# Reordering the opening of a two-block transformer kernel: zero products first, half-unit weights, meta tokens turned raw

## The chip, the cores and the metric

The kernel runs on one core of a Trainium2 chip. The metric is the device time of one execution in microseconds (us). The profiled execution also has a span, the time from its first to its last instruction.

## The reference

Two transformer blocks run over 256 tokens of width 1024. Only the start of the first block matters here: 16 meta tokens are put ahead of the 256 tokens of x, the 272 rows are normed, and the result is multiplied by the weight matrix `w_in`.

```
h = concatenate([meta_tokens, x])          # 16 + 256 rows of 1024
a = h * rsqrt(mean(h*h, axis=-1) + EPS) * norm1
proj = a @ w_in                            # u, q, k, v of two attentions, forget gates
...                                        # pool mixer, two attentions, w_out, gated FFN
                                           # then the second block: FFN, convolution + mLSTM, FFN
```

## The kernel before

**Arithmetic.** Every float32 product with a large weight is made from two parts. A value is rounded to fp32r (its "hi" part), and what is left is its "lo" part. A result is hi·hi + hi·lo + lo·hi, three passes of TensorE. So weights are held as `raw`, `whi`, `wlo` and the activations as `xa`, with the hi part of a 128-column block `kt` at `xa[:, kt, 0:272]` and its lo part at `xa[:, kt, 272:544]`.

**Weights.** All large weights stream in as 1 MB units of 128 x 2048, each of which holds two output tiles (a = 0, 1) of eight 128 x 128 blocks, ordered by kt and then a. There are three slots. SyncE's queue loads a unit into `raw[slot]` once `lo_ready` says that the unit before it in that slot is split. ScalarE writes `whi` (`split`, L608), VectorE subtracts to get `wlo` (L911), TensorE uses both. `unit_used` counts units that TensorE is done with.

**The opening.** SyncE's queue issues x in two parts, the identity, the meta tokens, the vectors of gains, unit 0, `small` (gate and pool weights), unit 1, the constants, unit 2 (L547 to L555). ScalarE squares each part of x with a running sum and takes the root, VectorE scales the identity by 1/rms (`diag`, L963), and TensorE multiplies x by that diagonal, which turns x and norms it in one product (`turn_first`). That is a plain float32 product of 128 columns, which shows as two records in the trace. The meta tokens are squared on VectorE (L967) and turned in the same way with a 16 x 16 diagonal `diag_m`: eight small products, each behind the turn of one kt of the second part of x. Each kt has a PSUM bank of its own. Then ScalarE writes the hi part of `xa` with the gain `norm1` (L706), and VectorE the lo part (L984). VectorE alone splits unit 0: a cast to `whi` (L973), the lo part of tile 0 (L978, `half_ready`), and, after the lo parts of `xa`, the lo part of tile 1 (`lo_ready`).

**The first unit.** TensorE takes the work in the order of the list `FIRST`: tile 0 (`proj` 0) with `columns_tile`, three products of 272 columns for each kt, each kt behind its `xa_ready`; tile 1; then `gates` (24 small-weight products, which wait for `small_lo_ready`), then tiles 2 and 3 of unit 1, and so on. ScalarE copies an even tile out of PSUM bank 0, VectorE an odd one out of bank 1. All products are issued by one helper, `mm`, whose line is L1325.

## Time and profile before

| | |
|---|---|
| median of 3 runs | 844.18 us |
| lowest, highest run | 840.53, 844.36 us |
| profiled execution, its time | 842.73 us |
| its span | 840.9 us |
| mean granted TensorE clock | 0.986 |
| TensorE, VectorE, ScalarE busy | 97%, 64%, 51% |

1.83 us of the profiled execution's time lie outside its span. The granted clock is a share of TensorE's full 2.4 GHz, so 0.50 is 1.2 GHz. A busy TensorE isn't TensorE at its peak, since matmuls are pipelined and weight loads (PEld) lie beside them.

### The profile page before, as it was taken

Reading aid. Unit: us, or ns where it says so; the run is one execution under the profiler, and the core shown is the slowest. Engines: PE = TensorE matmul, PEld = TensorE weight load, DVE = VectorE, ACT = ScalarE, POOL = GpSimd, SP = SyncE. Lnnn points to the kernel's source line nnn. Section 1 sums busy time; section 2 is a strip of 40 time slices with the busy share of each in tenths; the row PEclk is TensorE's granted clock in tenths of the full one; section 3 lists DMA queues with packets and bytes.
Section 4 is the critical chain, followed back from the end, with each engine's and each line's share of the span. In section 5 each row is a group of like instructions: output and inputs, shape, how many; then the busy total and the mean of one; then the engine's idle time right before and its main releaser. Section 6 shows DMA issues by size and latency. Waiting matters only on the chain.

```text
span 840.9 us, 12339 instructions
## 1 busy us (share of the span) xinstructions
PE 815.0 (97%) x4807; PEld 715.3 (85%) x4807; DVE 538.0 (64%) x633; ACT 427.5 (51%) x553; POOL 19.7 (2%) x24
## 2 busy tenths in 40 slices
PE   6999997999999999999999999999999999999997
PEld 6989886888888888988888888899887988888886
DVE  5664523676665666786656665876778776666665
ACT  5356542754444445854444446635445754454444
POOL 0000000000000000000000000000440000000000
PEclk8999987999999999999999999999999999999999
DMA  6632122265555455465554554432335555555431
GB/s 259 253 121 101 57 95 100 98 226 183 194 200 193 176 183 196 141 237 196 200 185 176 189 198 163 163 151 101 114 137 201 178 218 184 194 200 193 175 131 50
DMA packets 20653, 141.07 MB, mean 168 GB/s; under 512 B 2432, under 2 KB 2688, under 8 KB 4112
## 3 DMA queue, kind: packets, MB, share of 16 engines
q1 hardware_dynamic: 20048, 138.56, 45.3%
q0 software_dynamic: 576, 2.10, 0.7%
q8 instruction: 21, 0.34, 0.2%
q14 instruction: 8, 0.07, 0.0%
HBM read 139.60 MB, written 1.05 MB: 167 GB/s over the span
## 4 chain that ended last, share of the span: by engine, by line
PE 85%; DVE 7%; ACT 4%; issue 2%; POOL 1%; DMA 1%; DVEq 0%; SPq 0%; ACTq 0%
PE ps L1325 84%; DVE wlo L911 2%; ACT whi L608 1%; PE ps L1331 1%; DMA ident<-ident_in 1%; DVE arena L1292 0%; DVE x L1090 0%; ACT squared L623 0%; DVE xa L922 0%; DVE sb_parts L1074 0%; PE ps L1526 0%; DVE arena L1072 0%; POOL arena L591 0%; DVE arena L1302 0%; ACT arena L879 0%
## 5 line engine op out<-in xcount | busy, mean ns | idle before, releaser
L1325 PE MATMUL ps<-xa,whi 128*128 128x512 f32 (+2 forms) x1808 | 505.0, 348 | 0.8 <-DVE ytmp L1262 0.8
L1325 PE MATMUL ps<-xa,wlo 128*128 128x256 f32 (+1 forms) x1408 | 395.3, 283 | 0.0
L911 DVE TENSOR_TENSOR wlo<-raw,whi 128x2048 fp32r<-128x2048 f32 x128 | 294.1, 2298 | 103.1 <-ACT whi L608 103.0
L1325 PEld LDWEIGHTS ps<-xa,whi 128*128 128x128 f32 x1808 | 315.8, 190 | 45.5 <-issue 3.0
L1325 PEld LDWEIGHTS ps<-xa,wlo 128*128 128x128 f32 x1408 | 267.0, 190 | 1.1
L608 ACT ACTIVATE whi<-raw 128x2048 fp32r<-128x2048 f32 x128 | 244.2, 1908 | 12.1 <-PE ps L1325 11.9
L1325 PE MATMUL ps<-whi,hhi 128*128 128x512 f32 x240 | 93.8, 391 | 0.0
L1325 PE MATMUL ps<-whi,hlo 128*128 128x512 f32 x240 | 93.7, 390 | 0.0
L1325 PE MATMUL ps<-wlo,hhi 128*128 128x512 f32 x240 | 93.5, 390 | 0.0
L794 ACT ACTIVATE hhi<-arena 128x512 fp32r<-128x512 f32 x30 | 19.0, 633 | 89.0 <-PE ps L1325 82.5
L780 ACT ACTIVATE arena<-ps 128x512 f32<-128x512 f32 x33 | 19.7, 596 | 87.5 <-PE ps L1325 87.3
L1325 PE MATMUL ps<-whi,ya 128*128 128x512 f32 x176 | 58.4, 406 | 1.5 <-DVE arena L1254 1.5
L788 ACT ACTIVATE arena<-ps 128x512 f32<-128x512 f32 x33 | 19.7, 596 | 73.1 <-PE ps L1325 73.1
L1325 PEld LDWEIGHTS ps<-whi,hlo 128*128 128x128 f32 x240 | 45.1, 188 | 9.8
L1325 PEld LDWEIGHTS ps<-whi,hhi 128*128 128x128 f32 x240 | 45.1, 188 | 9.6
L1325 PEld LDWEIGHTS ps<-wlo,hhi 128*128 128x128 f32 x240 | 45.1, 188 | 8.5
L1132 DVE TENSOR_TENSOR arena<-ps,arena 128x512 f32<-128x512 f32 x33 | 22.8, 690 | 41.6 <-ACT arena L780 41.6
L1141 DVE TENSOR_TENSOR arena<-ps,arena 128x512 f32<-128x512 f32 x33 | 22.8, 690 | 38.7 <-ACT arena L788 38.6
L1153 DVE TENSOR_TENSOR hlo<-arena,hhi 128x512 fp32r<-128x512 f32 x30 | 20.8, 693 | 38.4 <-ACT hhi L794 38.4
L1325 PEld LDWEIGHTS ps<-whi,ya 128*128 128x128 f32 x176 | 34.0, 193 | 8.9 <-DVE arena L1254 1.8
L1325 PE MATMUL ps<-wlo,ya 128*128 128x512 f32 x88 | 35.1, 399 | 0.0
L1325 PE MATMUL ps<-arena 128*64 128x256 f32 (+9 forms) x180 | 25.6, 337 | 0.8 <-DVE arena L1023 0.5
(190 smaller groups left out, 531.3 us busy)
## 6 DMA issues: line engine op xcount, KB each, us to landing
raw<-wstream SPq DMA_DIRECT2D x129, 1024.0 KB, 4.8
gain_row<-rows_in POOLq DMA_DIRECT2D x4, 512.0 KB, 4.2
x<-x_in SPq DMA_DIRECT2D x2, 512.0 KB, 4.0
out<-x SPq DMA_DIRECT2D x4, 256.0 KB, 2.1
xg<-const_in SPq DMA_DIRECT2D x1, 840.0 KB, 9.4
small<-small_in SPq DMA_DIRECT2D x1, 152.0 KB, 5.8
ident<-ident_in SPq DMA_DIRECT2D x1, 64.0 KB, 4.4
arena<-meta_in SPq DMA_DIRECT2D x1, 64.0 KB, 4.4
```

Source lines behind the costliest of these rows:

```text
L608: nc.scalar.activation(whi[slot][:], raw[slot][:], ACT.Copy).then_inc(hi_ready, 1)
L780: nc.scalar.activation(silu, products(4)[1], ACT.Copy).then_inc(gate_lo_out, 1)
L788: nc.scalar.activation(up_sum, products(6)[1], ACT.Copy).then_inc(up_lo_out, 1)
L794: nc.scalar.activation(ya[:, 0:2, 0:SEQ] if last else hhi[:], hact, ACT.Copy).then_inc(hhi_done, 1)
L911: nc.vector.tensor_tensor(wlo[slot][:], raw[slot][:], whi[slot][:].bitcast(F32), ALU.subtract).then_inc(lo_ready, 1)
L1132: nc.vector.tensor_tensor(silu, products(4)[0], silu, ALU.add).then_inc(gate_out, 1)
L1141: nc.vector.tensor_tensor(up_sum, products(6)[0], up_sum, ALU.add).then_inc(up_out, 1)
L1153: nc.vector.tensor_tensor(lo, hact, hi.bitcast(F32), ALU.subtract).then_inc(hlo_done, 1)
L1325: return nc.tensor.matmul(o, lhsT, rhs, start=start, stop=stop, skip_group_check=True)
L1331: ins = nc.tensor.transpose(turn_place(k, kt)[:, tt * P:(tt + 1) * P], x[:, tt, kt * P:(kt + 1) * P], ident[:])
```

## The change

- Before anything else TensorE makes 12 float32 products of 128 columns from a buffer of zeros (`vn[0][:, 0]`), which VectorE now clears second. Their result, in PSUM bank 0, isn't read.
- The meta tokens are turned raw, as eight transposes into one bank, right behind the zeros. VectorE multiplies them by `norm1` in one instruction, and later, in one instruction for hi and two for lo, by their 1/rms. That reaches all partitions through one product of ones with `diag_m` (`meta_spread`).
- The scaled identities are made by ScalarE, not by VectorE. The turned x lies in banks 3 to 6, two kt to a bank; `norm_turned` now counts pairs of kt.
- SyncE's queue issues the meta tokens ahead of the identity, unit 0 in two halves (kt 0 to 3, kt 4 to 7, both tiles in each), and unit 2 ahead of the constants. VectorE splits each half.
- `first_unit` replaces the first two calls of `columns_tile`: the products with the hi part of `xa` for both tiles first (kt 0 to 3, then kt 4 to 7), those with its lo part last.
- `small` is split ahead of unit 1 on both engines.

Declarations of semaphores are left out of the diff.

```diff
@@ -311,6 +311,9 @@
         xm = carve(at, D)[0:META, :]
...
         diag_m = carve(at, META)[0:META, :]
+        meta_gained = carve(at, KT, META)
+        meta_scaled = carve(at, KT, META)
+        ones_first = carve(at, P)[0:META, :]
         at = [0]
         qT = [carve(at, PAIRS, SEQ) for _ in range(2)]
@@ -512,6 +522,10 @@
             else:
                 engine.wait_ge(m_taken[n % 2], n // 2 + 1)
+        def first_turn_place(kt):
+            return ps[:, 3 + kt // 2, kt % 2 * SEQ:(kt % 2 + 1) * SEQ]
         def in_place(what, s, j):
             if what == "k":
@@ -545,14 +559,15 @@
         def _(sp):
...
                 sp.dma_start(x[:, tt, :], x_in[tt * P:(tt + 1) * P, :]).then_inc(x_landed[tt], 16)
+            sp.dma_start(xm, meta_in).then_inc(meta_landed, 16)
             sp.dma_start(ident[:], ident_in).then_inc(ident_landed, 16)
-            sp.dma_start(xm, meta_in).then_inc(meta_landed, 16)
             sp.dma_start(vecs[:], vecs_in).then_inc(vecs_landed, 16)
-            sp.dma_start(raw[0][:], wstream[0]).then_inc(landed[0], 16)
+            sp.dma_start(raw[0][:, 0:UNIT // 2], wstream[0, :, 0:UNIT // 2]).then_inc(half_landed, 16)
+            sp.dma_start(raw[0][:, UNIT // 2:UNIT], wstream[0, :, UNIT // 2:UNIT]).then_inc(landed[0], 16)
             sp.dma_start(small[:], small_in).then_inc(small_landed, 16)
             sp.dma_start(raw[1][:], wstream[1]).then_inc(landed[1], 16)
+            sp.dma_start(raw[2][:], wstream[2]).then_inc(landed[2], 16)
             sp.dma_start(const_raw, const_in).then_inc(const_landed, 16)
-            sp.dma_start(raw[2][:], wstream[2]).then_inc(landed[2], 16)
             with sp.Fori(1, UNITS // SLOTS) as turn:
                 for s in range(SLOTS):
@@ -650,7 +665,7 @@
             def hi_of(k, gain, tiles):
                 for kt in tiles:
-                    act.wait_ge(norm_turned, KT + 4 * k + turn_group(kt) + 1)
+                    act.wait_ge(norm_turned, KT // 2 + 4 * k + turn_group(kt) + 1)
                     nc.scalar.activation(xa[:, kt, 0:SEQ], turn_place(k, kt), ACT.Copy, scale=vec(gain, kt)).then_inc(xa_hi_ready, 1)
             def root_of_x(p, tt):
@@ -697,18 +712,20 @@
                 act.wait_ge(x_landed[tt], 16)
...
                 root(1, tt, False)
+                act.wait_ge(root_ready, tt + 1)
+                act.wait_ge(ident_landed, 16)
+                nc.scalar.activation(diag[:, tt, :], ident[:], ACT.Copy, scale=stat[:, 20 + tt:21 + tt]).then_inc(diag_ready, 1)
             act.wait_ge(meta_squared, 1)
...
             for kt in range(KT):
-                act.wait_ge(norm_turned, kt + 1)
-                nc.scalar.activation(xa[:, kt, 0:TOK], ps[:, kt, 0:TOK], ACT.Copy,
+                act.wait_ge(norm_turned, kt // 2 + 1)
+                nc.scalar.activation(xa[:, kt, META:TOK], first_turn_place(kt), ACT.Copy,
                                      scale=vec("norm1", kt)).then_inc(xa_hi_ready, 1)
-            split(1, 1, 0)
             act.wait_ge(small_landed, 16)
             nc.scalar.activation(small_hi[:], small[:, 0:W_POOL], ACT.Copy).then_inc(small_hi_ready, 1)
+            split(1, 1, 0)
             for kind, i in FIRST:
                 b45 = 4 + i % 2
@@ -952,43 +969,53 @@
             nc.vector.memset(eps[:], EPS).then_inc(eps_set, 1)
+            nc.vector.memset(vn[0][:, 0, :], 0.0).then_inc(zeros_set, 1)
+            nc.vector.memset(ones_first, 1.0).then_inc(ones_set, 1)
             nc.vector.memset(kT[1][:, :, TOK:3 * P], 0.0)
             nc.vector.memset(fneg, 0.0)
-            nc.vector.memset(vn[0][:, 0, :], 0.0)
             nc.vector.memset(vn[1][:, 2, :], 0.0)
-            dve.wait_ge(ident_landed, 16)
-            def diagonal(tt):
-                dve.wait_ge(root_ready, tt + 1)
-                nc.vector.tensor_scalar(diag[:, tt, :], ident[:], stat[:, 20 + tt:21 + tt], None, ALU.mult).then_inc(diag_ready, 1)
-            diagonal(0)
             dve.wait_ge(meta_landed, 16)
...
                                            accum_out=stat[0:META, 30:31]).then_inc(meta_squared, 1)
-            diagonal(1)
+            dve.wait_ge(meta_turned, 1)
+            dve.wait_ge(vecs_landed, 16)
+            norm1 = vec("norm1", 0, KT).unsqueeze(2).broadcast_to([P, KT, META])
+            nc.vector.tensor_tensor(meta_gained, ps[:, 7, 0:KT * META].rearrange("p (k m) -> p k m", k=KT), norm1, ALU.mult)
+            def first_hi_part(n):
+                part = slice(n * UNIT // 2, (n + 1) * UNIT // 2)
+                dve.wait_ge(landed[0] if n else half_landed, 16)
+                nc.vector.tensor_copy(whi[0][:, part], raw[0][:, part]).then_inc(first_hi, 1)
+            def first_lo_part(n):
+                part = slice(n * UNIT // 2, (n + 1) * UNIT // 2)
+                dve.wait_ge(first_hi, n + 1)
+                nc.vector.tensor_tensor(wlo[0][:, part], raw[0][:, part], whi[0][:, part].bitcast(F32),
+                                        ALU.subtract).then_inc(lo_ready if n else half_ready, 1)
+            first_hi_part(0)
+            first_lo_part(0)
+            dve.wait_ge(ident_landed, 16)
             dve.wait_ge(root_ready, 3)
             nc.vector.tensor_scalar(diag_m, ident[0:META, 0:META], stat[0:META, 32:33], None, ALU.mult).then_inc(diag_ready, 1)
-            dve.wait_ge(landed[0], 16)
-            link(nc.vector.tensor_copy(whi[0][:], raw[0][:]))
-            def rest_of_first(a):
-                part = lambda w: w.rearrange("p (k a n) -> p k a n", k=KT, a=2)[:, :, a, :]
-                return nc.vector.tensor_tensor(part(wlo[0][:]), part(raw[0][:]), part(whi[0][:].bitcast(F32)), ALU.subtract)
-            rest_of_first(0).then_inc(half_ready, 1)
-            dve.wait_ge(vecs_landed, 16)
+            first_hi_part(1)
+            dve.wait_ge(meta_spread, 1)
+            meta_rstd = ps[:, 2, 0:META].unsqueeze(1).broadcast_to([P, KT, META])
+            nc.vector.tensor_tensor(xa[:, :, 0:META], meta_gained, meta_rstd, ALU.mult).then_inc(xa_meta_ready, 1)
+            link(nc.vector.tensor_tensor(meta_scaled, meta_gained, meta_rstd, ALU.mult))
+            nc.vector.tensor_tensor(xa[:, :, TOK:TOK + META], meta_scaled, xa[:, :, 0:META].bitcast(F32),
+                                    ALU.subtract).then_inc(xa_meta_ready, 1)
+            first_lo_part(1)
             for kt in range(KT):
-                dve.wait_ge(xa_hi_ready, kt + 1)
-                nc.vector.scalar_tensor_tensor(xa[:, kt, TOK:2 * TOK], ps[:, kt, 0:TOK], vec("norm1", kt),
-                                               xa[:, kt, 0:TOK].bitcast(F32), ALU.mult,
+                dve.wait_ge(xa_hi_ready, kt // 2 * 2 + 2)
+                nc.vector.scalar_tensor_tensor(xa[:, kt, TOK + META:2 * TOK], first_turn_place(kt), vec("norm1", kt),
+                                               xa[:, kt, META:TOK].bitcast(F32), ALU.mult,
                                                ALU.subtract).then_inc(xa_ready, 1)
-            rest_of_first(1).then_inc(lo_ready, 1)
-            split(1, 1)
             dve.wait_ge(small_hi_ready, 1)
...
                                     ALU.subtract).then_inc(small_lo_ready, 1)
+            split(1, 1)
             for kind, i in FIRST:
                 b45 = 4 + i % 2
@@ -1104,7 +1131,7 @@
             def normed_x():
                 dve.wait_ge(gain_landed, 16)
-                dve.wait_ge(norm_turned, KT + 4 + turn_group(KT - 1) + 1)
+                dve.wait_ge(norm_turned, KT // 2 + 4 + turn_group(KT - 1) + 1)
                 for tt, h in HALVES:
...
                     nc.vector.scalar_tensor_tensor(half(x, tt, h), half(x, tt, h), stat[:, 8 + tt:9 + tt],
@@ -1347,11 +1374,9 @@
                     ins = mm(ps[:, bank, tt * P:(tt + 1) * P], ones, diag[:, tt, :], True, True)
                 ins.then_inc(rstd_spread, 1)
-            def columns_tile(o, slot, a, n, first_wait=None, skip=0):
+            def columns_tile(o, slot, a, n, skip=0):
                 for kt in range(KT):
-                    if first_wait is not None:
-                        pe.wait_ge(xa_ready, first_wait + kt + 1)
                     w = slice(kt * 256 + a * P, kt * 256 + (a + 1) * P)
...
                     mm(o, whi[slot][:, w], xa[:, kt, n + skip:2 * n], False, False)
@@ -1441,16 +1466,61 @@
                 return ins
-            def turn_first(tt, kt):
-                return mm(ps[:, kt, META + tt * P:META + (tt + 1) * P], x[:, tt, kt * P:(kt + 1) * P], diag[:, tt, :], True, True)
+            def turn_first(tt, tiles):
+                for kt in tiles:
+                    ins = mm(first_turn_place(kt)[:, tt * P:(tt + 1) * P], x[:, tt, kt * P:(kt + 1) * P], diag[:, tt, :], True, True)
+                    if tt and kt % 2:
+                        ins.then_inc(norm_turned, 1)
+            def first_unit():
+                def product(kt, a, part, lo, stop=False):
+                    w = slice(kt * 256 + a * P, kt * 256 + (a + 1) * P)
+                    return mm(ps[:, a, 0:TOK], part[0][:, w], xa[:, kt, lo * TOK:(lo + 1) * TOK], kt == 0 and part is whi and not lo, stop)
+                pe.wait_ge(xa_meta_ready, 1)
+                pe.wait_ge(half_ready, 1)
+                for kt in range(KT // 2):
+                    pe.wait_ge(xa_hi_ready, kt + 1)
+                    for part in (whi, wlo):
+                        for a in range(2):
+                            product(kt, a, part, 0)
+                pe.wait_ge(first_hi, 2)
+                for kt in range(KT // 2, KT):
+                    pe.wait_ge(xa_hi_ready, kt + 1)
+                    for a in range(2):
+                        product(kt, a, whi, 0)
+                pe.wait_ge(lo_ready, 1)
+                for kt in range(KT // 2, KT):
+                    for a in range(2):
+                        product(kt, a, wlo, 0)
+                pe.wait_ge(xa_meta_ready, 2)
+                for kt in range(KT - 1):
+                    pe.wait_ge(xa_ready, kt + 1)
+                    for a in range(2):
+                        product(kt, a, whi, 1)
+                pe.wait_ge(xa_ready, KT)
+                product(KT - 1, 0, whi, 1, True).then_inc(even_full, 1)
+                product(KT - 1, 1, whi, 1, True).then_inc(unit_used, 1)
+            pe.wait_ge(zeros_set, 1)
+            for _ in range(12):
+                mm(ps[:, 0, 0:P], vn[0][:, 0, 0:P], vn[0][:, 0, P:2 * P], True, True)
+            pe.wait_ge(meta_landed, 16)
+            pe.wait_ge(ident_landed, 16)
+            for kt in range(KT):
+                ins = nc.tensor.transpose(ps[:, 7, kt * META:(kt + 1) * META], xm[:, kt * P:(kt + 1) * P], ident[0:META, 0:META])
+            ins.then_inc(meta_turned, 1)
             pe.wait_ge(diag_ready, 1)
-            for kt in range(KT):
-                turn_first(0, kt)
+            turn_first(0, range(KT))
+            pe.wait_ge(diag_ready, 2)
+            turn_first(1, range(KT // 2))
+            pe.wait_ge(ones_set, 1)
             pe.wait_ge(diag_ready, 3)
-            for kt in range(KT):
-                turn_first(1, kt)
-                mm(ps[:, kt, 0:META], xm[:, kt * P:(kt + 1) * P], diag_m, True, True).then_inc(norm_turned, 1)
+            mm(ps[:, 2, 0:META], ones_first, diag_m, True, True).then_inc(meta_spread, 1)
+            turn_first(1, range(KT // 2, KT))
             for kind, i in FIRST:
                 pair = 6 + i % 2
@@ -1460,16 +1530,13 @@
                     n = U_IN + i // 2
...
                     if i == 0:
-                        pe.wait_ge(half_ready, 1)
-                    if i == 1:
-                        pe.wait_ge(xa_ready, KT)
-                        pe.wait_ge(lo_ready, 1)
+                        first_unit()
                     if i >= 2:
...
                         wait_tiles(pe, i - 2)
-                    skip = META if query else 0
-                    columns_tile(ps[:, i % 2, skip:TOK], n % SLOTS, i % 2, TOK, 0 if i == 0 else None,
-                                 skip).then_inc(unit_used if i % 2 else even_full, 1)
+                        skip = META if query else 0
+                        columns_tile(ps[:, i % 2, skip:TOK], n % SLOTS, i % 2, TOK,
+                                     skip).then_inc(unit_used if i % 2 else even_full, 1)
                 if kind == "gates":
...
```

## Rows read from the trace of the kernel before

**Rows 1.** The profile's page: busy time, share of the span, instructions.

```profile
PE 815.0 (97%) x4807; PEld 715.3 (85%) x4807; DVE 538.0 (64%) x633; ACT 427.5 (51%) x553; POOL 19.7 (2%) x24
```

**Rows 2.** Waits of TensorE, whole span: us in total, times, longest.

```profile
PE ps L1325 <- DVE sb_parts L1074: 7.2, 3, 4.7
PE ps L1325 <- DVE diag L963: 6.5, 1, 6.5
```

**Rows 3.** Windows: length, PE, PEld, DVE, ACT, POOL busy, PEclk, DMA share, GB/s.

```profile
6.47:14.60 8.13, 8.13 (x39) 7.15 (x39) 6.10 (x10) 3.79 (x11) 0.00 (x0) 1.00 1.01 417
14.70:21.40 6.70, 6.70 (x27) 6.14 (x28) 4.58 (x6) 4.77 (x7) 0.00 (x0) 0.50 0.17 53
21.50:25.20 3.70, 3.70 (x32) 3.70 (x31) 3.20 (x3) 0.86 (x2) 0.00 (x0) 1.00 0.96 385
105.00:110.00 5.00, 3.94 (x21) 3.94 (x22) 1.34 (x2) 0.11 (x1) 0.00 (x0) 0.68 0.46 187
```

**Rows 4.** Timeline of the opening, VectorE: start, length, what.

```profile
1.68 0.38 DVE L957 MEMSET arena<- 128x384 f32 x1
...
6.13 0.29 DVE L963 TENSOR_SCALAR diag<-ident,stat 128x128 f32<-128x128 f32 x1 [3.66 <-DMA ident<-ident_in]
...
6.50 1.21 DVE L967 SCALAR_TENSOR_TENSOR arena<-arena 16x1024 f32<-16x1024 f32 x1
...
7.66 0.27 DVE L963 TENSOR_SCALAR diag<-ident,stat 128x128 f32<-128x128 f32 x1
...
8.96 1.23 DVE L973 CAST whi<-raw 128x2048 fp32r<-128x2048 f32 x1 [0.42 <-DMA raw<-wstream]
10.22 1.22 DVE L978 TENSOR_TENSOR wlo<-raw,whi 128x1024 fp32r<-128x1024 f32 x1
...
13.29 0.50 DVE L984 SCALAR_TENSOR_TENSOR xa<-ps,vecs,xa 128x272 fp32r<-128x272 f32 x1 [0.24 <-ACT xa L706]
```

**Rows 5.** Timeline of the opening, TensorE: turning x and the meta tokens.

```profile
6.47 4.21 PE L1325 MATMUL ps<-diag,x 128*128 128x128 f32 x18 [6.47 <-DVE diag L963]
...
11.92 0.49 PE L1325 MATMUL ps<-diag,x 128*128 128x128 f32 x2
...
12.34 0.39 PE L1325 MATMUL ps<-arena 16*128 16x16 f32 x2
...
15.01 0.80 PE L1325 MATMUL ps<-diag,x 128*128 128x128 f32 x2
...
15.73 0.60 PE L1325 MATMUL ps<-arena 16*128 16x16 f32 x2
...
17.53 0.82 PE L1325 MATMUL ps<-xa,whi 128*128 128x272 f32 x2
```

**Rows 6.** Timeline, TensorE: products of the first unit, then the gates.

```profile
18.15 0.43 PE L1325 MATMUL ps<-xa,wlo 128*128 128x272 f32 x1
...
18.83 0.43 PE L1325 MATMUL ps<-xa,wlo 128*128 128x272 f32 x1
...
22.27 0.29 PE L1325 MATMUL ps<-xa,wlo 128*128 128x272 f32 x1
...
24.14 0.29 PE L1325 MATMUL ps<-xa,wlo 128*128 128x272 f32 x1
...
25.27 0.21 PEld L1325 LDWEIGHTS ps<-xa,small_hi 128*6 128x6 f32 x2
```

**Rows 7.** Timeline and lines: turns by transpose, 6 and 128 rows.

```profile
34.31 0.31 PE L1481 MATMUL ps<-ident,arena 6*128 6x6 f32 x3
...
L1526 PE MATMUL ps<-ident,arena 128*128 128x128 f32 x8 | 1.1, 279 | 0.6 <-ACT arena L739 0.6
```

**Rows 8.** DMA issues: size in KB, median us to landing.

```profile
ident<-ident_in SPq DMA_DIRECT2D x1, 64.0 KB, 4.4
```

**Rows 9.** Timeline: what VectorE does as the first unit ends.

```profile
22.42 2.28 DVE L911 TENSOR_TENSOR wlo<-raw,whi 128x2048 fp32r<-128x2048 f32 x1
...
25.59 0.44 DVE L1023 COPY arena<-ps 128x272 f32<-128x272 f32 x1 [0.89 <-PE ps L1325]
```

More of the change, by code:

```diff
@@ L407, in build_blocks @@
         meta_squared = sem("meta_squared")
+        zeros_set = sem("zeros_set")
+        ones_set = sem("ones_set")
+        half_landed = sem("first_half_unit_landed")
+        first_hi = sem("first_unit_hi_ready")
+        meta_turned = sem("meta_turned")
+        meta_spread = sem("meta_rstd_spread")
+        xa_meta_ready = sem("xa_meta_columns_ready")
         diag_ready = sem("diag_ready")
```

## The prediction

> **What bounds the kernel now.** I read the page first. TensorE is busy for 97% of the span [rows 1], so anything that ends a stretch of TensorE earlier moves the end of the kernel, provided nothing later hangs on another clock. Next the waits of TensorE: over the whole span they hold two large entries, 7.2 us in the attention of the first block and 6.5 us in the very first wait, for the scaled identity [rows 2]. Only the second is in the reach of this change. Third, the windows of the opening. The reader is to look at PEclk, the granted clock: it is 1.00 up to 14.6 us, 0.50 from 14.7 to 21.4 and 1.00 again from 21.5 [rows 3]. So the opening has two losses: TensorE idle until 6.47, and then 6.8 us at 1.2 GHz in which it was busy all the time. What did it do before the clock fell? It had idled for 6.5 us, and then made float32 products of 128 columns, at last mixed with 16 x 16 ones [rows 5]. Before the clock rose it had made products of 272 columns from 17.53 on [rows 5]. A later fall, between 105 and 110 us, follows a wait [rows 2, 3]. So both thin work and idling precede falls here, and the rows can't say which of them made the one at 14.65.
>
> The point at which I compare is the first weight load of the gates, at 25.27 [rows 6]. From there on TensorE has the same list of work.
>
> **What TensorE's opening becomes.** I write the new order out with prices of the rows.
>
> *Zeros.* The clear of the zero buffer starts at 1.68 now, and two clears of about 0.4 us stand ahead of it that move behind it. So it starts at 0.9, lasts 0.38 [rows 4] and lets TensorE go at 1.3. A float32 product of 128 columns is two records; 18 records took 4.21 us [rows 5], so a product costs 0.468 at the full clock. 12 x 0.468 = 5.6: the zeros end at 6.95. They are no longer under cover to their end: the first scaled identity was ready at 6.42 [rows 4], so some 0.5 us of them is on the path. Bounds for one product are 0.42 (a turn up to the meta product behind it, 12.34 - 11.92) and 0.72 (the same at the lower clock, 15.73 - 15.01) [rows 5].
>
> *Meta tokens raw.* Eight transposes of 16 rows. Meta tokens and identity now leave the queue third and fourth, so the identity is due some 0.45 us later than its 6.1 (it took 4.4 from issue [rows 8]), before 6.95. The trace has three transposes of 6 rows in 0.31 us and eight of 128 rows in 1.1 [rows 7]; I take 0.8 for the eight, since the 16-row ones resemble the first, with 1.1 as the upper bound. End: 7.75.
>
> *Turns of x.* 16 x 0.468 = 7.5, and one small product for the spread of the meta roots, 0.39 (the pair of meta records, with its tail [rows 5]). Seven such products are gone. End of turning: 7.75 + 7.5 + 0.39 = 15.6, against 17.53. ScalarE makes both identities; VectorE had them at 6.4 and 7.9 [rows 4]. On ScalarE the second comes behind the square of the second x tile and a wait for its own root, which I put at 9.0, and TensorE asks for it at 11.5. Cover 2.5 us.
>
> *Products of the first unit.* Two tiles of 24 before, 32 + 16 now: 48 either way. At the full clock the products from 22.27 to 24.14 are 15, so 0.125 each; at the lower one three take 0.68, so 0.227 [rows 6]. 48 x 0.125 = 6.0. End: 21.6.
>
> Sum: 25.27 - 21.6 = 3.6 us earlier. About 2.9 of that is clock. Between 17.53 and 21.45 some 17.3 products cost 0.10 too much each, 1.8 us; and of the 2.9 us of turning after 14.65, 1.1 is clock, by the lengths 0.80 + 0.60 against 0.49 + 0.39 [rows 5]. The other 0.7 is reordered work. So the change lives on whether the clock stays up.
>
> **Are the operands there?** The products want the hi parts of `xa`. ScalarE can make kt 0 to 3 from about 12.6 on, as their pairs are turned, and kt 6 and 7 by 16.7, while TensorE asks for kt 6 at about 18.1. VectorE: square of the meta tokens 6.1 to 7.35 (1.21 [rows 4]); their gain at 7.8, when TensorE has turned them; the first half of unit 0, landed before the whole of it at 8.96, cast in 0.6 (half of 1.23) and its remainder in 1.22 [rows 4], by 10.0; second half cast by 10.9. Then VectorE waits for `meta_spread`. That is a new wait: TensorE gets to it only at 13.8, and behind it on VectorE stand the second half's lo part and all lo parts of `xa`. Three small instructions bring it to 14.5, the lo part (1.22) to 15.7, eight lo parts of `xa` at 0.5 each [rows 4] to 19.7. TensorE wants the second half's lo part at 18.6, and the last lo part of `xa` at 15.6 + 46 x 0.125 = 21.4. Slack 1.7 us. Price if the cover were gone: VectorE's lateness one for one.
>
> **What follows it.** The gates need `small_lo`, which comes right behind, at 20.1. Splitting unit 1 then ends on VectorE at 22.4, tile 2 starts at 24.6. VectorE splits unit 2 until 24.7, as now (22.42 + 2.28), so its copy of the odd tile comes at 24.7 instead of 25.59 [rows 9]; tile 3 needs bank 1 at 27.5. Slack 2.8. ScalarE's copy of tile 0 moves from inside the unit to its end, 21.7, and bank 0 is wanted at 24.6. SyncE's queue has one issue more, but the transfers run at 417 GB/s through 14.6 us [rows 3], so bytes and not issues set the landings; the constants land one unit later and are read by ScalarE near 29. Unit 3 is asked for when unit 0 is split, 15.7 instead of 20. I cost all of these at nothing, and give each a chance below only through VectorE.
>
> **A rule weighed.** The Trainium skill ("TensorE: Matmul & The Clock Gate", Part 1) says that the default state is the lower clock and that activity releases it. This trace disagrees at the start: the first products, after 6.5 us of idling, ran at 1.00. By the rule the zeros would warm the clock up; by the row there is nothing to warm, and the zeros can only keep. The skill also says there (Part 4) that transposes in TensorE's transpose mode don't count as busy in the same way; it speaks against putting the eight of them ahead of the turns, and no row here shows it.
>
> **Against the runs.** The profiled execution took 842.73, span 840.9. The four executions shown (844.36, 844.18, 840.53, 842.73) average 842.95, and their spread of 3.8 is as large as the gain. I take 842.95 - 3.6 = 839.3. That is 4.9 under the median of 844.18, 0.58%. A measurement of this kernel tells about 0.5% (4.2 us) from no change, so the forecast stands just past the bound.
>
> **The rivals.**
> - *The clock still falls near the end of the turning*, as at 14.65. For: the turns stay thin work, and thin work stood right before the fall. Against: the 16-column products, the thinnest, are gone from there, and there is no idling ahead. Price: the last 0.95 us of turning is 1.54 times as long (0.72 / 0.468), 0.5; then the products run for 3.95 us at the lower clock, as from 17.53 to 21.45, 17.4 of them at 0.10 too much, 1.8. Gain 3.6 - 2.3 = 1.3: 841.6. If it falls at 12.1 the gain is gone: 843.
> - *VectorE becomes the bound* through the wait for `meta_spread`. For: five jobs are queued behind it. Against: 1.7 us of slack. If its small instructions and waits cost 2.7 more than I think, 1.0 is lost: 840.3.
> - *The lower clock from the first zeros on.* One mechanism, slower: a product of zeros, or a program whose first act is thin work at 1.3 us, draws the fall to the start. Zeros 12 x 0.72 to 9.9, transposes 1.6, turns 11.5, spread 0.6: 23.6; 3.95 us of products at 0.227, then 30.6 at 0.125: 31.4. That is 6.1 late: 849.1. It is slower than before once the fall comes ahead of 12.1, and measurably so ahead of about 4. For: idling and thin work precede the falls. Against: thin work from 6.47 to 10.6 ran at 1.00 [rows 3, 5]. By the rule of the skill cited above, a start at the lower clock is the default.
>
> **Chances.** Clock stays up, 839.3: 0.55. Late fall, 841.6: 0.25. VectorE, 840.3: 0.10. Fall near 12, no change: 0.06. Lower clock from the start, 849.1: 0.04. The range runs from the lowest run shown less the gain (840.53 - 3.6 = 836.9) to the fall near 12 (843.0). Price bounds lie inside: zeros at 0.42 give 0.6 more, transposes at 1.1 take 0.3. Against the median, faster by over 0.5% means under 839.96. The first case does it in some 0.63 of its executions' spread (0.35), the second seldom (0.05), the third in half (0.05): 0.45. Slower by over 0.5%: 0.04. The rest, 0.51, lies within.
>
> **What the new profile would show.** Windows: PEclk 1.00 from 0 to 22; a 0.50 there is one of the clock rivals, and its start says which. Timeline of TensorE: zeros 1.3 to 6.95, first product of unit 0 at 15.6, first gate load at 21.6. Waits: none of TensorE on VectorE between 15 and 22. The prediction is wrong if the first gate load comes at 21.6 and the time doesn't follow; then a later fall of the clock, shifted or added, has taken it back.

## Result: 834.76 us against 844.27, ratio 0.9891, and the profile after

Four runs each gave a median of 834.76 us (831.78 to 835.33) for the changed kernel and 844.27 (840.53 to 844.65) for the one before: ratio 0.9891, 95% interval 0.9862 to 0.9919, so 7 to 12 us less by the interval. I had forecast 839.3, at least 836.9. The profiled execution took 835.33 with a span of 833.1. The direction was right, and the gain that I had forecast at the gates was less than half of what came.

The first thing to read is again the first weight load of the gates. This is the timeline of the changed kernel on TensorE up to there (start, length, what):

```profile
1.36 5.44 PE L1352 MATMUL ps<-arena 128*128 128x128 f32 x24 [1.36 <-DVE arena L972]
6.72 0.67 PE L1514 MATMUL ps<-ident,arena 16*128 16x16 f32 x8
7.32 2.94 PE L1352 MATMUL ps<-diag,x 128*128 128x128 f32 x24
10.47 0.36 PE L1352 MATMUL ps<-arena 16*128 16x16 f32 x2 [0.21 <-DVE arena L1001]
10.76 1.16 PE L1352 MATMUL ps<-diag,x 128*128 128x128 f32 x8
11.68 0.49 PE L1352 MATMUL ps<-xa,whi 128*128 128x272 f32 x2
...
15.78 2.16 PE L1352 MATMUL ps<-xa,whi 128*128 128x272 f32 x16
17.77 0.41 PE L1352 MATMUL ps<-xa,small_hi 128*6 128x272 f32 x2
```

The gates' products begin at 17.77; in the timeline the products of the kernel before begin at 25.39, 0.12 behind the weight load of [rows 6]. That is 7.6 us earlier, where I had 3.6. The terms of the sum: zeros to 6.8 (I had 6.95), transposes 0.67 (0.8), unit 0 in 6.0 us (6.0). The turns are the odd one. 24 records took 2.94 us and 8 took 1.16 with its tail, 0.122 a record, so 0.245 for a turn (two records). I had 0.468, nearly twice that. And the zeros, the same kind of product, did take 0.453 each.

The windows of the changed kernel (columns as in [rows 3]):

```profile
0.00:25.00 25.00, 23.44 (x174) 22.14 (x175) 17.39 (x33) 16.07 (x30) 0.86 (x5) 1.00 0.87 330
95.00:110.00 15.00, 12.82 (x81) 12.04 (x81) 7.15 (x9) 4.86 (x8) 0.00 (x0) 0.77 0.24 94
120.00:135.00 15.00, 10.29 (x46) 8.73 (x46) 7.00 (x8) 2.82 (x3) 0.00 (x0) 0.66 0.20 70
```

PEclk is 1.00 through the opening: the fall at 14.65 is gone, as the first case of the forecast had it. Two later falls, of which [rows 3] show one for the kernel before, are still there.

The waits of TensorE up to 20 us (us in total, times, longest):

```profile
PE ps L1352 <- DVE arena L972: 1.4, 1, 1.4
PE ps L1352 <- DVE arena L1001: 0.2, 1, 0.2
```

The 6.5 us of [rows 2] have become 1.4, for the cleared buffer, and there is a new wait of 0.2 for `diag_m` (L1001). The timeline of VectorE in the changed kernel shows where that comes from:

```profile
8.24 0.69 DVE L989 CAST whi<-raw 128x1024 fp32r<-128x1024 f32 x1 [0.49 <-DMA raw<-wstream]
8.97 1.23 DVE L994 TENSOR_TENSOR wlo<-raw,whi 128x1024 fp32r<-128x1024 f32 x1
10.11 0.22 DVE L1001 TENSOR_SCALAR arena<-ident,stat 16x16 f32<-16x16 f32 x1
10.25 0.67 DVE L989 CAST whi<-raw 128x1024 fp32r<-128x1024 f32 x1
...
11.60 1.22 DVE L994 TENSOR_TENSOR wlo<-raw,whi 128x1024 fp32r<-128x1024 f32 x1
12.73 3.22 DVE L1012 SCALAR_TENSOR_TENSOR xa<-ps,vecs,xa 128x256 fp32r<-128x256 f32 x8
15.87 0.33 DVE L1016 TENSOR_TENSOR small_lo<-small,small_hi 128x176 fp32r<-128x176 f32 x1
...
20.52 0.43 DVE L1050 COPY arena<-ps 128x272 f32<-128x272 f32 x1
```

`diag_m` stands behind the cast and the remainder of the first half. The last lo part of `xa` is there at 15.95, and its product runs near 17.6: the slack of 1.7 us, as forecast.

**Where the factor of two was.** In the opening the length of a weight load tells the clock better than PEclk does. Here are the groups of weight loads, by shape, in four stretches (count, busy us, mean ns). First the kernel before, 6.47 to 10.5 us:

```profile
L1325 PEld LDWEIGHTS ps<-diag,x 128*128 128x128 f32 x18 | 3.9, 330 | 6.5 <-DVE diag L963 6.5
```

The same kernel, 11.1 to 14.5:

```profile
L1325 PEld LDWEIGHTS ps<-diag,x 128*128 128x128 f32 x10 | 1.5, 192 | 0.1
```

The changed kernel, zeros (1.36 to 6.3), then turns (7.3 to 11.5):

```profile
L1352 PEld LDWEIGHTS ps<-arena 128*128 128x128 f32 x24 | 5.2, 331 | 1.4 <-DVE arena L972 1.4
```

```profile
L1352 PEld LDWEIGHTS ps<-diag,x 128*128 128x128 f32 x31 | 3.6, 191 | 0.1
```

A weight load of 128 columns takes 330 ns at first and 191 ns later, in both kernels, and 1.00 is what PEclk shows for all four stretches. 330 is the length that goes with 1.2 GHz, as the kernel before shows between 17.7 and 21.3, where PEclk is 0.50 and recorded:

```profile
L1325 PEld LDWEIGHTS ps<-xa,whi 128*128 128x128 f32 x12 | 3.3, 327 | 0.0
```

So TensorE began at the lower clock in both kernels, and the 1.00 ahead of the first recorded change isn't a measurement. The clock records kept in the two traces say the same: the first one, of the full clock, begins at 11.25 us in the kernel before and at 6.62 in the changed one, and for the time ahead of it there is none. PEclk counts time without a record as 1.00.

The trace of the kernel before also held the price of such a product at the full clock, in a later stretch that I hadn't looked at, behind several recorded changes. Two float32 products of 128 columns (four records) stand there one behind the other:

```profile
172.60 0.61 PE L1325 MATMUL ps<-diag,exact 128*128 128x128 f32 x4
```

That is 0.31 us a product at most, with the tail of the last one in it.

### The profile page after: what moved, and what is told of

The parts are those of the page before. It is cut to its first block, busy times and chain, and to the rows that moved or that the text cites. A ratio compares the mean times of both kernels' runs of the same rounds, so it can differ in the third digit from the quotient of the medians.

```text
span 833.1 us, 12387 instructions
## 1 busy us (share of the span) xinstructions
PE 812.1 (97%) x4825; PEld 713.6 (86%) x4825; DVE 537.7 (65%) x637; ACT 428.0 (51%) x555; POOL 19.7 (2%) x24
## 4 chain that ended last, share of the span: by engine, by line
PE 85%; DVE 7%; ACT 4%; issue 2%; POOL 1%; DMA 1%; SPq 0%; DVEq 0%; ACTq 0%
PE ps L1352 84%; DVE wlo L928 2%; ACT whi L623 1%; PE ps L1358 1%; DMA raw<-wstream 1%; DVE arena L1319 0%; DVE x L1117 0%; ACT squared L638 0%; DVE xa L939 0%; DVE sb_parts L1101 0%; PE ps L1593 0%; DVE arena L1099 0%; POOL arena L606 0%; DVE arena L1329 0%; ACT arena L896 0%
## 5 line engine op out<-in xcount | busy, mean ns | idle before, releaser
L1352 PE MATMUL ps<-arena 128*64 128x256 f32 (+10 forms) x190 | 27.5, 349 | 2.3 <-DVE arena L972 1.4
```

What stands on the lines that cost most here:

```text
L1352: return nc.tensor.matmul(o, lhsT, rhs, start=start, stop=stop, skip_group_check=True)
```

## The experiments

All times are medians of several runs; ratios are against the kernel before, run on the same chip in turn. "Gates" is the first weight load of the gates in the profiled execution (25.27 before; 17.66 in the changed kernel, 0.11 ahead of the product above). Five profiled executions whose opening is in effect that of the changed kernel (the changed one twice, 9, 11, 13) have it between 17.59 and 17.84, so a difference under 0.3 us at the gates says little.

**1. No zeros.** The changed kernel without its opening products.

```diff
-            for _ in range(12):
-                mm(ps[:, 0, 0:P], vn[0][:, 0, 0:P], vn[0][:, 0, P:2 * P], True, True)
```

> The changed kernel without its 12 products of zeros. Theory (TensorE was at the lower clock in its first products in both kernels, whatever PEclk shows, and the zeros take that time out of the turns): weight loads of 333 ns in the first turns; transposes 1.3 us instead of 0.67, some six turns at 0.455 us and ten at 0.245, so the turning ends near 13.4 instead of 11.68 and the gates begin near 19.4 instead of 17.77; if the clock then falls as it did in the kernel before, up to 3 us more, so 21 to 22.5. Rival (the turns became fast by themselves, because nothing stands between them any more): turns at 0.245 from the first on, gates at 17.8 or a little earlier, time equal to that of the changed kernel.

Measured: 837.50 us, ratio 0.9934 (0.9912 to 0.9955). The weight loads of the turns between 7.6 and 11 us:

```profile
L1352 PEld LDWEIGHTS ps<-diag,x 128*128 128x128 f32 x16 | 3.5, 330 | 0.0
```

They were slow again. Turning ended at 13.60, gates at 19.58, PEclk stayed 1.00. The theory holds, the rival falls. The zeros are worth 1.9 us at the gates. They cost nothing there: without them TensorE starts its transposes at 6.72, as in the changed kernel, because the identity isn't there earlier.

```profile
6.72 1.00 PE L1512 MATMUL ps<-ident,arena 16*128 16x16 f32 x8 [6.72 <-DMA ident<-ident_in]
```

**2. Zeros only.** The kernel before with the zeros alone.

```diff
             nc.vector.memset(eps[:], EPS).then_inc(eps_set, 1)
+            nc.vector.memset(vn[0][:, 0, :], 0.0).then_inc(zeros_set, 1)
...
-            nc.vector.memset(vn[0][:, 0, :], 0.0)
...
+            pe.wait_ge(zeros_set, 1)
+            for _ in range(12):
+                mm(ps[:, 0, 0:P], vn[0][:, 0, 0:P], vn[0][:, 0, P:2 * P], True, True)
             pe.wait_ge(diag_ready, 1)
```

> The kernel before with nothing added but the 12 products of zeros (and the clear of their buffer moved ahead). Theory of the clock: eight turns at 0.245 from 6.85 on, then eight pairs of turn and meta product at about 0.6 to 0.74, end of turning 13.7 to 14.8 instead of 17.53, no fall of PEclk, unit of 6.0 us or a little more: gates near 20 to 21 instead of 25.27, 4 to 5 us of the 7.5 that the whole change gains. Rival (the gain is the reordering): the zeros only hold TensorE until 6.85, gates at 25.3 to 25.7, time not below the kernel before.

Measured: 840.43 us, ratio 0.9980 (0.9968 to 0.9992), gates at 21.83. Turning ended at 14.30 with short weight loads, as expected. But the clock fell then, which I hadn't expected and which put the gates past the 20 to 21 of the forecast; the window of the start of the unit:

```profile
14.00:18.20 4.20, 4.20 (x22) 4.17 (x22) 3.61 (x4) 3.95 (x5) 0.00 (x0) 0.59 0.47 162
```

So the zeros bring the clock up and don't by themselves keep it. What remains between them and the fall is the run of turns with 16-column products between. The median gains 2.1 us on the 842.50 of the kernel before beside it; the profiled execution (839.25) is one of the faster of twelve.

**3. Twenty-four zeros.**

```diff
-            for _ in range(12):
+            for _ in range(24):
```

> The changed kernel with 24 products of zeros instead of 12. Theory of the clock: one kind of record, no operand changes, and yet weight loads go from 333 ns to about 190 near 6 to 7 us while PEclk shows 1.00 before and after; the zeros end near 9.7, and the gates begin about 2.5 us later than 17.77. Rival (a record of zeros costs 0.227 us for a reason of its own, such as its operands): the second twelve cost 0.227 each record too, zeros end at 12.3, gates 5.3 us later.

Measured: 837.30 us, ratio 0.9935 (0.9917 to 0.9954), gates at 19.93, 2.3 us later. The same products, same operands, by shape, up to 6.1 us and from 6.9 on:

```profile
L1352 PEld LDWEIGHTS ps<-arena 128*128 128x128 f32 x23 | 5.0, 332 | 1.3 <-DVE arena L972 1.3
```

```profile
L1352 PEld LDWEIGHTS ps<-arena 128*128 128x128 f32 x20 | 2.3, 192 | 0.0
```

and PEclk over the same two stretches (columns as in [rows 3]):

```profile
1.35:6.10 4.75, 4.75 (x22) 4.75 (x23) 1.17 (x4) 2.31 (x5) 0.00 (x0) 1.00 0.91 297
6.90:9.30 2.40, 2.40 (x23) 2.28 (x21) 0.71 (x2) 2.27 (x8) 0.00 (x0) 1.00 1.01 388
```

The product and its operands are the same in both, and the load goes from 332 to 192 ns with PEclk at 1.00 on both sides. This is the cleanest evidence that the first PEclk isn't measured. The first clock record of this trace begins at 6.30.

**4. Tile by tile.** The changed kernel with unit 0 multiplied in the old order.

```diff
-                pe.wait_ge(xa_meta_ready, 1)
+                pe.wait_ge(xa_meta_ready, 2)
                 pe.wait_ge(half_ready, 1)
...
+                for a in range(2):
+                    for kt in range(KT):
+                        if a == 0:
+                            if kt == KT // 2:
+                                pe.wait_ge(first_hi, 2)
+                                pe.wait_ge(lo_ready, 1)
+                            pe.wait_ge(xa_ready, kt + 1)
                         product(kt, a, whi, 0)
...
                         product(kt, a, whi, 1)
...
+                        ins = product(kt, a, wlo, 0, kt == KT - 1)
+                    ins.then_inc(unit_used if a else even_full, 1)
```

> The changed kernel with the first unit in the old order: tile 0 whole, each kt behind its lo part of xa, then tile 1. If the order of products is worth something by itself: the first product waits for the lo part of kt 0 (13.1 instead of 11.68) and is paced by VectorE's 0.40 each, so the gates begin near 19.3, 1.5 us later. Rival (the operands are there in time anyway, as I costed it at nothing): gates within 0.3 us of 17.77.

Measured: 836.37 us, ratio 0.9930 (0.9909 to 0.9951), gates at 19.54, 1.9 later. TensorE waited for VectorE ahead of the first product (timeline):

```profile
13.52 0.49 PE L1352 MATMUL ps<-xa,whi 128*128 128x272 f32 x2 [1.44 <-DVE xa L1012]
```

The order of products matters: the first one can't start before the first lo part of `xa`, and tile 1 comes only after tile 0. (Some 0.2 us of the 1.9 is a later landing: VectorE's first cast began at 8.40 here and at 8.24 in the changed kernel.)

**5. Interleaved.** The changed kernel with a 16 x 16 product behind each turn of the second part of x; the results aren't used.

```diff
+                    if tt:
+                        ins = mm(ps[:, 0, 0:META], xm[:, kt * P:(kt + 1) * P], ident[0:META, 0:META], True, True)
```

> The changed kernel with a 16 x 16 product again behind each turn of the second part of x (eight added, results unused), zeros and everything else kept. Pace of such a pair at the full clock: 0.74 us instead of 0.245 per turn, so the turning ends near 15.6 instead of 11.68 and the gates begin near 21.7. Theory (the thin mix at the end of the turning is what drew PEclk to 0.50 in the kernel before): PEclk falls between 11 and 16 us although nothing idled, and the gates begin at 23 to 24.5. Rival (the fall came from the idling ahead of the first product, which the zeros have removed): PEclk stays 1.00, gates 21.7.

Measured: 842.01 us, ratio 0.9984 (0.9971 to 0.9998), gates at 24.13, nearly the whole gain gone. Its windows, and its first product of the unit (timeline):

```profile
12.00:13.20 1.20, 1.20 (x9) 1.02 (x9) 0.79 (x4) 0.84 (x2) 0.00 (x0) 1.00 1.01 430
13.50:20.00 6.50, 6.50 (x26) 5.92 (x26) 4.72 (x11) 4.17 (x7) 0.00 (x0) 0.50 0.81 321
```

```profile
16.57 0.82 PE L1352 MATMUL ps<-xa,whi 128*128 128x272 f32 x2
```

PEclk fell between 13.2 and 13.5, with TensorE busy since 1.35. The idling ahead of the first product wasn't needed for it; the rival falls. The fall is about half of the loss: the turn of kt 5 starts at 13.01, and three pairs at 0.74 from there would have put the first product at 15.2 and the gates near 21.2 (an estimate by the paces above). So some 3.5 us of the 6.5 is the slower pace of turns with 16-column products between, and some 3 is the clock. What in the mix draws the fall, the narrow products themselves or the lower use of the engine that comes with them, this run doesn't separate.

**6. Raw meta tokens only.** No zeros (as in 1) and the old order of products (as in 4).

> The changed kernel without the zeros and with the first unit in the old order, so what is left is the raw meta tokens, the turns one behind another, the halves and the order of loads. If the parts add: turning ends near 13.5, first product held by VectorE until about 14.5, no fall of PEclk, gates near 21, 4 us ahead of the kernel before; with the zeros (1.8) and the order of products (1.8) that makes the 7.5. Rival (without zeros the fall comes back): PEclk 0.50 in part of 14 to 22, gates near 23.

Measured: 839.08 us, ratio 0.9961 (0.9946 to 0.9976), gates at 21.08, no fall of PEclk. The parts nearly add: 25.27 - 21.08 = 4.2 for turning without 16-column products between and whatever else of the change this run keeps, 1.9 for the zeros (1), 1.9 for the order (4), 8.0 against 7.6 measured. Why 0.4 is counted twice no run shows.

**7. One landing.** Unit 0 in one transfer, still split in halves.

```diff
-            sp.dma_start(raw[0][:, 0:UNIT // 2], wstream[0, :, 0:UNIT // 2]).then_inc(half_landed, 16)
-            sp.dma_start(raw[0][:, UNIT // 2:UNIT], wstream[0, :, UNIT // 2:UNIT]).then_inc(landed[0], 16)
+            sp.dma_start(raw[0][:], wstream[0]).then_inc(landed[0], 16)
```

> The changed kernel with unit 0 loaded by one transfer, split in halves as before. The first cast on VectorE starts at 8.96 instead of 8.24 (landing as in the kernel before), VectorE's chain to diag_m and meta_spread is as much later, and TensorE waits for it: gates 0.5 to 0.8 us later, time at most 1 us above the changed kernel. Rival (landing is hidden): nothing.

Measured: 835.73 us, ratio 0.9915 (0.9897 to 0.9932), gates at 18.21, 0.55 later. TensorE's wait for `diag_m`, in its timeline:

```profile
11.02 0.36 PE L1351 MATMUL ps<-arena 16*128 16x16 f32 x2 [0.87 <-DVE arena L1000]
```

0.87 instead of 0.21. The half landing is worth 0.4 to 0.6 us at the gates; the time can't tell it from nothing.

**8. Six zeros.**

```diff
-            for _ in range(12):
+            for _ in range(6):
```

> The changed kernel with 6 products of zeros instead of 12. They end at 4.1 and TensorE idles until the identity lands at 6.6. If the zeros only help while they fill the time up to the turns: the first turns have weight loads of 333 ns, turning ends between 12 and 13.6, gates 0.5 to 1.8 us later. Rival (six are as good as twelve, since the clock has had its work): weight loads of 191 ns from the first turn on, gates at 17.8.

Measured: 837.49 us, ratio 0.9933 (0.9915 to 0.9951), gates at 18.81, 1.2 later. The gates lie in the range of the first theory, but by luck, since neither theory had the course of it. The zeros ended at 4.3, TensorE idled 2.3 us, and then:

```profile
7.13:8.30 1.17, 1.17 (x12) 1.17 (x11) 0.58 (x3) 1.12 (x3) 0.00 (x0) 1.00 0.94 358
8.50:11.70 3.20, 3.20 (x17) 2.98 (x15) 2.52 (x4) 1.78 (x7) 0.00 (x0) 0.50 1.04 419
```

```profile
L1352 PEld LDWEIGHTS ps<-diag,x 128*128 128x128 f32 x11 | 1.3, 191 | 0.0
```

The first turns were fast, so six zeros had brought the clock up; its first record begins at 5.00, while TensorE idled. Then it fell, with PEclk recorded this time, and stayed low for the rest of the first turns. So what the second six do is bridge the wait for the identity.

**9. Ones instead of zeros.** The opening products read a buffer of ones.

```diff
-            nc.vector.memset(vn[0][:, 0, :], 0.0).then_inc(zeros_set, 1)
+            nc.vector.memset(gain_row[:, 0:2 * P], 1.0).then_inc(zeros_set, 1)
...
+            nc.vector.memset(vn[0][:, 0, :], 0.0)
...
-                mm(ps[:, 0, 0:P], vn[0][:, 0, 0:P], vn[0][:, 0, P:2 * P], True, True)
+                mm(ps[:, 0, 0:P], gain_row[:, 0:P], gain_row[:, P:2 * P], True, True)
```

> The changed kernel with its 12 opening products made from a buffer of ones instead of zeros. If it is the activity of the engine and not the data that brings the clock up: the same, turns with weight loads of 191 ns, gates at 17.8, time as the changed kernel. Rival (zeros are weak work, ones bring the clock up earlier): the weight loads of the opening products turn fast well before 6 us in this run; a rise between 4 and 6.8 us is within what the runs with zeros showed.

Measured: 834.64 us, ratio 0.9891 (0.9871 to 0.9910), gates at 17.72, weight loads of 333 ns until past 6 us. Zeros or ones makes no difference here; other data wasn't tried.

**10. The changed kernel once more.**

> The changed kernel itself once more, beside the next two and in more runs. Gates at 17.8; time 834.5 to 835, so 8 us or 0.93% below the 842.5 that the kernel before has over its many runs (7.5 for the opening, the rest scatter of the later falls of the clock). Rival (the first comparison's 9.5 us holds, so there is a gain behind the opening too): 833 or less.

Measured: 833.94 us, ratio 0.9895 (0.9876 to 0.9914), gates at 17.84. The kernel before had 844.01 beside it, and 842.50 beside experiments 1 to 4. So the gain was 10 us here, and the 7.4 at the gates leave over 2 open. 833.94 lies between what my two theories gave and decides for neither.

**11. Fillers in the later waits.** The changed kernel with 8 and 19 products of constants ahead of two waits for `sb_parts` in the first block; results unused.

```diff
                 if kind == "sb_later":
+                    if i:
+                        pe.wait_ge(y_tmp, Y_AT[(None, ("fox_norm", 1), ("sb_norm", 0))[i]] + 1)
+                        for _ in range((0, 8, 19)[i]):
+                            mm(ps[:, pair, :], ident_r[:], exact[:, 0:512], True, True)
                     pe.wait_ge(sb_plus, i + 1)
```

> The changed kernel with filler products in the two long waits of TensorE for sb_parts in the first block (8 and 19 fp32r products of 512 columns of constants, results unused). Theory (PEclk falls near 98 and 122 us because TensorE idles 2.2 and 4.7 us there): both falls go, 12 to 18 us at the lower clock go with them, worth 4 to 6 us: 829 to 831. Rival (the work right behind the waits is thin itself, and draws the fall without the idling, or the fillers delay it): no more than 1 us gained.

Measured: 828.39 us (828.21 to 828.84), ratio 0.9832 (0.9815 to 0.9848). Windows over the two places, and the wait that is left:

```profile
96.00:106.00 10.00, 9.70 (x74) 8.49 (x73) 5.05 (x6) 4.86 (x8) 0.00 (x0) 1.00 0.32 105
120.00:132.00 12.00, 11.73 (x69) 9.42 (x68) 3.87 (x3) 4.15 (x4) 0.00 (x0) 1.00 0.29 114
```

```profile
PE ps L1352 <- DVE sb_parts L1101: 0.9, 3, 0.3
```

Both falls are gone, the waits that went into them are filled (0.9 us left of 7.2), and the time is 5.6 us below the median of experiment 10 and 6.4 below that of the first comparison, a little more than the forecast 4 to 6. The two kernels weren't run side by side; by their ratios to the kernel before the difference is 5 to 6 us. The runs lie within 0.6 us of each other, those of the changed kernel within 3.6: in the changed kernel the later falls were also the scatter.

**12 and 13. The kernel before with the same fillers, and the changed one again.**

> The kernel before with the filler products in the two long waits of the first block (8 and 19), opening untouched. If the opening is worth its 7.5 us at the gates and nothing behind it: 7.3 to 8 us above the changed kernel with the same fillers in the same call, so 835.5 to 836.5, with scatter under 1 us in both, since the later falls are gone. Rival (the change also gains 1 to 3 us behind the opening, by something other than the falls at 100 and 125 us): a difference of 9 us or more. Second rival (the surplus over 7.5 is the later falls, which the changed kernel meets at luckier times): difference 7.5 here, against 8 to 10 without fillers.

> The changed kernel with the fillers, once more, as the partner of the run above: 828.2 to 828.8, PEclk 1.00 throughout. It should beat both the kernel before and the changed kernel (by 5 to 6 us).

Measured: 836.02 us (834.99 to 838.72), ratio 0.9914 (0.9898 to 0.9929), and 828.31 (828.22 to 828.61), ratio 0.9827 (0.9814 to 0.9840). The difference is 7.7, as forecast, so no gain behind the opening shows. The scatter under 1 us that I had expected of both came only in the changed kernel; the kernel before, with its old opening, still scatters by 3.7. The profiled execution of the former was its slowest, 838.72, and shows a third way through the old opening. Its window, and the weight loads of unit 0 by shape from 19.9 to 23.9:

```profile
0.00:30.00 30.00, 23.60 (x108) 21.01 (x109) 16.30 (x25) 13.21 (x23) 0.86 (x5) 1.00 0.68 262
```

```profile
L1325 PEld LDWEIGHTS ps<-xa,whi 128*128 128x128 f32 x12 | 3.3, 327 | 0.0
L1325 PEld LDWEIGHTS ps<-xa,wlo 128*128 128x128 f32 x6 | 2.0, 330 | 0.0
```

Here the clock had not come up at all until past 24 (its first record begins at 25.51), the gates began at 28.38, and PEclk shows 1.00 for all of it. So the old opening costs 7.6 us over the new one in one kind of execution and 10.8 in another.

**All profiled executions in one table.** Time less the start of the gates is what lies behind the opening. The last column is PEclk over the window from 90 to 140 us, where the two later falls lie.

| kernel | gates | time | time less gates | PEclk, 90 to 140 |
|---|---|---|---|---|
| before | 25.27 | 842.73 | 817.5 | 0.84 |
| interleaved | 24.13 | 841.89 | 817.8 | 0.83 |
| zeros only | 21.83 | 839.25 | 817.4 | 0.83 |
| raw meta tokens only | 21.08 | 839.19 | 818.1 | 0.83 |
| 24 zeros | 19.93 | 837.90 | 818.0 | 0.83 |
| no zeros | 19.58 | 837.03 | 817.5 | 0.83 |
| tile by tile | 19.54 | 833.49 | 814.0 | 0.93 |
| 6 zeros | 18.81 | 836.83 | 818.0 | 0.83 |
| one landing | 18.21 | 834.49 | 816.3 | 0.86 |
| changed, once more | 17.84 | 833.94 | 816.1 | 0.86 |
| ones | 17.72 | 835.29 | 817.6 | 0.83 |
| changed | 17.66 | 835.33 | 817.7 | 0.83 |
| before, filled | 28.38 | 838.72 | 810.3 | 1.00 |
| changed, filled | 17.59 | 828.31 | 810.7 | 1.00 |
| changed, filled again | 17.61 | 828.31 | 810.7 | 1.00 |

Time less gates is one number, 817 to 818, wherever PEclk over that window is 0.83 or 0.84. It is 816 in the two rows with 0.86, 814 in the one with 0.93, and 810 to 811 in the three with fillers and 1.00. So what scatters behind the opening is the later falls; the row with 0.93 hasn't the first of them, though the same wait of 2.17 us stands there, so such a wait doesn't draw a fall each time.

## Why the prediction was wrong

**The step that failed** is the price of a turn: "a product costs 0.468 at the full clock". It costs 0.245 there. 0.468 was its price at 1.2 GHz, and I had taken it from a stretch where PEclk shows 1.00. Sixteen turns at 0.22 too much are 3.6 of the 3.9 us by which the turning ended ahead of my 15.6, at 11.68. The other terms held: zeros to 6.8 (6.95), transposes 0.67 (0.8), unit 6.0 (6.0). That of the zeros held by luck: 0.468 fits them because they ran at the lower clock. And the 0.5 us of zeros that I had put on the path isn't there, since TensorE starts at 6.72 without them too (1). Put into my sum, the measured 7.6 at the gates gives 842.95 - 7.6 = 835.3, against 834.76 measured.

**The rule weighed against the row** went the wrong way for the same reason. I wrote that by the row "there is nothing to warm, and the zeros can only keep". Experiments 1, 3 and 9 show that there was: weight loads go from 332 to 192 ns within one run of equal products. The Trainium skill ("TensorE: Matmul & The Clock Gate", Part 1) says that the default is the lower clock and activity releases it; by that rule, the trace agrees, once it is read by durations. The trace of before showed it. [rows 5] put a turn at 0.42 behind 11.92 and at 0.468 ahead of 10.6, and I took the smaller one for a bound instead of asking why the same product had two lengths; the weight loads by stretch, shown above, answer that at once. Even 0.42 isn't the price of turns one behind another, because a 16-column product followed each of those; the row at 172.60, 0.31 at most, comes near it.

**The rival of the lower clock** was half right: the zeros did run at 1.2 GHz from the first on. But no thin work had drawn a fall there, since the kernel before starts low too, and without zeros. Its price was wrong, since it let the turns stay low as well, and the zeros are what ends that.

**The forecast that PEclk stays up** was right, and experiments 2, 5 and 6 show why. With 16-column products between the turns it fell, without zeros (the kernel before) and with them (2, 5); with the turns one behind another it did not, with zeros or without (1, 3, 4, 6). Only a gap ahead of them, in 8, brought a fall of its own. (In 12 there was nothing to fall from.) The profiles are one execution each, but the other runs go with them: the mean granted clock is 0.983 to 0.988 in all 22 runs of 2 and 5 and 0.988 to 0.995 in all 27 of 1, 3, 4 and 6. What TensorE did before the fall in the kernel before was that mixture; the idling ahead of it played no part that shows. I had called it undecidable from the rows, which it was, and counted the removal of the idling as a reason too.

**VectorE's wait for `meta_spread`** was there as foreseen, with slack behind it. The wait that did reach TensorE was the one before it, 0.2 us for `diag_m`, because TensorE got there at 10.3 and not at 13.8. The order of products, which has no term of its own in the sum, is worth 1.7 to 1.9 us. That isn't a matter of the short turns. By the prediction's own times the lo parts of `xa` come from 16.2 to 19.7, so in the old order tile 0 would have ended at 20.1 and tile 1 at 23.1, not 21.6.

**What followed** was right: the shift reaches the end whole (table above). The medians moved by more than the gates, 9.5 and 10.1 us in the two comparisons, and the likely reason is that the kernel before passes through its opening in more than one way. That this is the whole of the surplus is argued, not shown. One profile caught the late rise. Of the 52 runs of the kernel before that stand beside the experiments, the 11 with a mean granted clock of 0.989 to 0.991 took 843.9 to 845.6; the other 41, with 0.985 to 0.988, took 840.5 to 843.8, but for one of 844.8. A clock that is recorded as low for a shorter time and a longer run fit together if a low stretch came before the first record.

**The range** was too narrow because its bounds for a product, 0.42 and 0.72, both came from turns with a 16-column product behind them, and the lower clock of the 0.468 between them went unseen.

## What to carry to other kernels

Ahead of the first recorded change, read TensorE's clock from the length of a weight load of known shape, and not from the granted clock; here two lengths for one shape and one operation meant two clocks. In an opening that waits for data, products whose result nobody reads (zeros and ones did it here) can fill the wait and bring the clock up, if they last until the real work starts and if nothing narrow is mixed into that work. And when a price decides a sum, look for the same instruction in a stretch where the clock is recorded, before taking it from one where it isn't.

## What the hardware showed that I had not expected

- PEclk of 1.00 while weight loads took 330 ns, that is 1.2 GHz: up to 6 us in experiment 3, and over the unit's products up to 23.9 us in experiment 12.
- With unread products from 1.2 or 1.35 us on, the clock rose at different times in executions of nearly the same code. The loads from 5 to 6 us average 192 ns in experiment 2 and are 333 ns past 6 us in experiment 9; the first clock records begin at 4.31 and 7.36. With the old opening they begin at 11.25 in one profile and 25.51 in the other.
- In experiment 8 the clock fell between 8.3 and 8.5 us, with TensorE busy again since 6.56 behind 2.3 us of idling.
- Two waits of 2.2 and 4.7 us in the middle of a kernel cost 5 to 6 us besides their own length: filled with useless work they last as long, and the kernel is 5 to 6 us shorter and scatters by 0.6 us instead of 3.6. The kernel with both changes, at 828.3, beats both kernels of this study.
